# The first turn of an experts' loop written out ahead of it, and its end laid out anew, in a decoder step on one Trainium2 core

## The chip, the core and the metric

The kernel runs on one core of one Trainium2 chip. Its engines run side by side, each with its own list of instructions: TensorE (PE; its weight loads are listed apart as PEld), VectorE (DVE), ScalarE (ACT), GpSimd (POOL) and SyncE (SP), which here only issues DMAs. They wait for each other by semaphores. The metric is the device time of one execution in microseconds, as the median of several runs.

## What is computed

The reference is one step of a hybrid decoder layer for 256 prompt tokens and 64 sample tokens (8 sequences of 8): adaptive norm, an input projection, retention and mLSTM heads, an output projection, then a mixture of experts. What matters here is the last part:

```python
logits = x @ w_router + b_router              # 320 tokens, 32 experts
gates = softmax(top_4(logits))
for e in range(32):                           # the tokens that chose expert e
    hu = xe @ w_up[e] + b_up[e]               # 1024 -> 2048
    gate, lin = min(hu[:, :1024], 7), clip(hu[:, 1024:], -7, 7)
    y = ((lin + 1) * gate * sigmoid(1.702 * gate)) @ w_down[e] + b_down[e]
    out[tokens] += gates[tokens, e] * y
x = x + gt_f * out                            # per token scale
y_final = rms_norm(x, g_final)
```

All 32 experts' weights, 12 MB each in float32, are read from HBM once.

## The kernel before

Before the loop, TensorE and the other engines do norm, projections, heads and router, and leave the normed tokens as three bfloat16 parts (`h2p`) whose sum is the float32 value. `counts_i` holds how many tokens chose each expert. The work of an expert is built for four sizes, 32, 64, 96 or 128 token slots; `by_size` compares the count and jumps to one of four copies of the code.

**The loop** runs over the experts as one body of code per engine (`expert` of TensorE at L1117, called at L1210). On TensorE a turn `e` is: the down product of expert `e - 2` (L1063; `BEHIND` is 2, so that the first two turns leave it out by a branch at L1119), two count loads, the up product of expert `e` (L1039: 4 pieces of w_up, for each piece the matmuls of L1048, then the bias matmuls of L1052), the gather of expert `e + 1` (`gather`, L1001: 72 matmuls of L1008 that pick the chosen tokens with a one-hot matrix, in a copy for up to 64 slots and one for 128), the scatter of expert `e - 2` into the token order (L1106), the turning of the activations (L1058) and of the gate weights (L1114). In turns 0 and 1, in which there is nothing to scatter, `fill` (L513) puts 14 or 3 matmuls without use in its place (L1136). A float32 matmul of the code is two records in the trace: the up product of 32 slots is 64 records of L1048 and 4 of L1052, that of 96 slots 192 and 12. The code of 64 and of 128 slots has as many matmuls as that of 32.

The first gather is a routine of its own (`gather_first`, L985), ordered by the arrival of the parts, 9 groups of 8 matmuls. After it TensorE waits for `counts_ready` and enters the loop.

**SyncE** issues the weights in an order that is written out by hand (L465 to L479): all of expert 0, w_up of expert 1, then in turn `e` the four w_up pieces of expert `e` (`load_ups`, 2 MB each) and the four w_down pieces of expert `e - 1` (`load_downs`, 1 MB each). There is one place for each piece, so each issue waits until the product that last read this place is done: w_up of expert 1 for the up product of turn 0, w_up of expert 2 for that of turn 1, w_down of expert 1 for the down product of expert 0, which runs in turn 2.

**ScalarE** in a turn makes the sigmoid, copies the gathered tokens (`copy_gathered`, L1479), the gate weights (`copy_weights`, L1515), the turned activations to `actT` (`copy_turned`, L1499, which waits until the down product before has read `actT`) and the down product's result to `yd` (L1530).

**The end.** After the loop TensorE runs the down product of expert 30 (L1212) into banks 6 and 7, and `last_expert` (L1166): the gate weights of expert 31, its down product into the same banks, hence after ScalarE has copied `yd`. Halfway through this product it does the scatter of expert 30 (`scatter_before`, L1172: samples, then the two prompt tiles). When it is done, VectorE and ScalarE copy the result out, and the scatter of expert 31 follows: samples (L1188), then tiles 0 and 1 (L1193). VectorE's `finish` (L2207) adds the three tiles to the residual, the samples first, and after all three scales each by its `rstd` and `g_final` (L2240); ScalarE sums the squares (L1546), GpSimd makes the `rstd` (L1598, L1599), SyncE stores each tile. The `g_final` load (L1541) is issued by ScalarE after its copies.

Of the kernel before, what the change touches and what calls it, by code (L numbers as in the profile page):

```python
# [13 lines left out]
D = 1024  # L14
# [71 lines left out]
def build(nc, a):  # L86
# [6 lines left out]
    with ctx:  # L93
# [128 lines left out]
        yd_last = at(2 * SLOT, 2, 512); G_last = at(2 * SLOT + D, NTOK)  # L222
        assert o5 + 7168 + 1536 <= WORDS, o5 + 8704
# [284 lines left out]
        def _(pe):  # L508
# [475 lines left out]

            def gather_first():  # L985
# [13 lines left out]
                last.then_inc(S("gathered"), 1)  # L999

            def gather(i, count, turned, e=None):  # L1001
# [12 lines left out]
                if count is None:  # L1014
                    products(128)
                    return
# [46 lines left out]
            def down(it, slots, meanwhile=None):  # L1063

                end = meanwhile is not None
# [9 lines left out]
                for u in range(2):  # L1075
                    pe.matmul(psum[0:slots, 6 + u, :], bsel_down[:, 0:slots],
                              bparts[:, 2 * D + 512 * u:2 * D + 512 * u + 512], start=True, stop=False)
                last = [None] * DOWN
                for j in range(pieces):
                    if end and j == pieces // 2:  # L1080
                        meanwhile()
                    for u in range(2):
                        for q in range(tiles):
                            piece = q * pieces + j
                            c = piece // 2
                            if slots == 96:
                                turned = actT.rearrange("p j s -> p (j s)")[:, 0:8 * slots] \
                                    .rearrange("p (j s) -> p j s", j=KD)[:, piece, :]
                            else:
                                turned = actT[:, j, slots * q:slots * q + slots]  # L1090
# [5 lines left out]
                            last[c] = pe.matmul(psum[slots * q:slots * q + slots, 6 + u, :], turned,  # L1096
# [19 lines left out]

            def expert(e):  # L1117
# [48 lines left out]
            def last_expert(its, count):  # L1166
# [3 lines left out]
                turn_weights(its, 1)  # L1170

                def scatter_before():  # L1172

                    pe.wait_ge(S("G_ready"), its + 1)
                    pe.wait_ge(S("y_copied"), its + 1)
                    for u in range(2):
                        pe.matmul(psum[64 * u:64 * u + 64, 0, :], G[:, tok(2)], yd[:, u, :], start=True, stop=False)
                    pe.wait_ge(S("y_gated"), 2)
                    for t in range(2):
                        for u in range(2):  # L1180
                            pe.matmul(psum[:, 2 + 2 * t + u, :], G[:, tok(t)], yd_gated[:, u, :], start=True, stop=False)

                pe.wait_ge(S("y_copied"), its + 1)
                by_size(pe, count, lambda slots: down(its - 1, slots, scatter_before))
                pe.wait_ge(S("G_ready"), its + 2)
                for u in range(2):
                    pe.wait_ge(S("y_copied"), its + 2 + u)
                    last = pe.matmul(psum[64 * u:64 * u + 64, 0, :], G_last[:, tok(2)], yd_last[:, u, :], start=False, stop=True)  # L1188
                last.then_inc(S("last_scattered"), 1)
                pe.wait_ge(S("y_gated"), 4)  # L1190
                for t in range(2):
                    for u in range(2):
                        last = pe.matmul(psum[:, 2 + 2 * t + u, :], G_last[:, tok(t)], yd_last_gated[:, u, :], start=False, stop=True)  # L1193
                    last.then_inc(S("last_scattered"), 1)
# [4 lines left out]
            gather_first()  # L1199
            pe.wait_ge(S("counts_ready"), 1)  # L1200

# [4 lines left out]
            def count_at(i):  # L1206
                where = slice(i, i + 1) if isinstance(i, int) else bass.ds(i, 1)
                return pe.value_load(counts_i[0:1, where], min_val=0, max_val=NTOK)

            with pe.Fori(0, NE) as e:  # L1210
                expert(e)
            by_size(pe, count_at(NE - 1), lambda slots: down(NE - 2, slots))  # L1212
            most = pe.value_load(counts_i[0:1, NE + 2:NE + 3], min_val=0, max_val=NTOK)
            with pe.If(most <= BIG_BLOCK):
                last_expert(NE, count_at(NE))
            with pe.Else():
# [5 lines left out]
                last_expert(NE * ROUNDS, None)  # L1222
# [3 lines left out]
        def _(act):  # L1226
# [272 lines left out]
            def copy_turned(it, slots, down_before):  # L1499
# [3 lines left out]
                if down_before:  # L1503
                    for c in range(DOWN):
                        act.wait_ge(piece_done[UP + c], it)
                if slots == 96:
                    by_piece = actT.rearrange("p j s -> p (j s)")[:, 0:n] \
# [5 lines left out]
                act.copy(actT.rearrange("p j s -> p (j s)")[:, 0:n], src).then_inc(S("actT_ready"), 1)  # L1513
# [12 lines left out]
            def expert(r, e, it, count, count_next):  # L1526
                take_up(r * (NE + 1) + e, it, count, count_next)
                copy_weights(it)
                by_size(act, count, lambda slots: copy_turned(it, slots, True))
                act.copy(yd.rearrange("p u n -> p (u n)"), flat(6, D)).then_inc(S("y_copied"), 1)  # L1530

            def last_expert(its):

                act.wait_ge(S("Pg_turned"), its + 1)
                act.copy(G_last, psum[:, 1, 0:NTOK]).then_inc(S("G_ready"), 1)
                for c in range(DOWN):
                    act.wait_ge(piece_done[c], its + 1)
                act.copy(yd_last[:, 0, :], psum[:, 6, :]).then_inc(S("y_copied"), 1)
                act.wait_ge(S("y_gated"), 3)
                act.copy(yd_last[:, 1, :], psum[:, 7, :]).then_inc(S("y_copied"), 1)  # L1540
                act.dma_start(gfin.rearrange("p u n -> p (u n)"), a["g_final"].partition_broadcast(128))\  # L1541
                    .then_inc(S("gfin_in"), 16)
# [20 lines left out]
            by_size(act, count, lambda slots: copy_turned(0, slots, False))  # L1563
# [6 lines left out]
            with act.Else():  # L1570
                with act.Fori(1, ROUNDS) as r:
# [166 lines left out]
        def _(dve):  # L1738
# [468 lines left out]
            def finish(its):  # L2207
# [16 lines left out]
                TT(yd_last_gated[:, 1, :], psum[:, 7, :], gateF_p[:, 512:D], ALU.mult).then_inc(S("y_gated"), 1)  # L2224
# [8 lines left out]
                for t in range(2):  # L2233
                    dve.wait_ge(S("last_scattered"), 2 + t)
                    TT(x2[:, t, :], x2[:, t, :], flat(2 + 2 * t, D), ALU.add).then_inc(S("x3_ready"), 1)
                dve.wait_ge(S("gfin_in"), 16)
                for i, t in enumerate(LAST_ORDER):
# [3 lines left out]
                        ALU.mult, ALU.mult).then_inc(S("y_final"), 1)  # L2241

# [93 lines left out]
```

## Time and profile before

| what | us |
|---|---|
| median of 3 runs | 1298.41 (1296.67 to 1298.94) |
| the profiled execution, its own time | 1295.37 |
| its span, first to last instruction | 1293.6 |
| TensorE busy | 1163.6 (90%) |
| VectorE, ScalarE, GpSimd busy | 375.8, 182.7, 72.0 |
| HBM read over the span | 459.78 MB, 360 GB/s |

In the rows below, times count from the start of the span. A row of the timeline has the start, the length, the engine, the line of the kernel, the operation, the tiles and the count; in brackets the idle time of the engine ahead of it and who ended it, where "issue" is time in which it waited for nothing that the profile shows. The granted clock of TensorE has two levels here, 1.00 and 0.50 of full speed. Branches and register loads are not in the rows.

### The profile page before, as it was taken

Reading aid. Unit: us, or ns where it says so; the run is one execution under the profiler, and the core shown is the slowest. Engines: PE = TensorE matmul, PEld = TensorE weight load, DVE = VectorE, ACT = ScalarE, POOL = GpSimd, SP = SyncE. Lnnn points to the kernel's source line nnn. Section 1 sums busy time; section 2 is a strip of 40 time slices with the busy share of each in tenths; the row PEclk is TensorE's granted clock in tenths of the full one; section 3 lists DMA queues with packets and bytes.
Section 4 is the critical chain, followed back from the end, with each engine's and each line's share of the span. In section 5 each row is a group of like instructions: output and inputs, shape, how many; then the busy total and the mean of one; then the engine's idle time right before and its main releaser. Section 6 shows DMA issues by size and latency. Waiting matters only on the chain.

```text
span 1293.6 us, 23349 instructions
## 1 busy us (share of the span) xinstructions
PE 1163.6 (90%) x8690; PEld 567.3 (44%) x8691; DVE 375.8 (29%) x819; ACT 182.7 (14%) x358; POOL 72.0 (6%) x178
## 2 busy tenths in 40 slices
PE   5999999996989999998999998999777889988986
PEld 4655447544335446443344544444223334343332
DVE  0164214848211222321222121142211221222235
ACT  3112232213010111110110110010100000110101
POOL 1010001431000000000000000000000000000001
PEclk9999999998899999998999999999879999989999
DMA  9944635883689999999999999999999999999992
GB/s 366 363 152 172 239 131 196 253 317 138 260 351 424 409 417 427 427 428 425 428 424 426 426 426 428 426 376 428 427 426 428 426 425 426 426 426 428 427 422 85
DMA packets 62481, 467.36 MB, mean 361 GB/s; under 512 B 6538, under 2 KB 24910, under 8 KB 26730
## 3 DMA queue, kind: packets, MB, share of 16 engines
q1 hardware_dynamic: 59770, 461.86, 86.7%
q10 hardware_dynamic: 2288, 4.37, 1.1%
q0 software_dynamic: 384, 0.59, 0.2%
q8 instruction: 28, 0.46, 0.1%
q14 instruction: 11, 0.09, 0.0%
HBM read 459.78 MB, written 6.42 MB: 360 GB/s over the span
## 4 chain that ended last, share of the span: by engine, by line
PE 58%; DMA 36%; DVE 2%; issue 2%; ACT 1%; POOL 0%; SPq 0%; ACTq 0%; POOLq 0%; DVEq 0%
DMA mem<-in_w_up 33%; PE psum L1048 20%; PE psum L1096 9%; PE psum L680 6%; PE psum L1106 5%; PE psum L661 3%; PE psum L1008 3%; PE psum L867 2%; PE psum L684 2%; DMA mem<-in_in_chunks 1%; PE psum L536 1%; DMA mem<-in_mod_chunks 1%; PE psum L1058 1%; PE psum L871 1%; PE psum L1052 1%
## 5 line engine op out<-in xcount | busy, mean ns | idle before, releaser
L1048 PE MATMUL psum<-mem 128*32 128x512 f32 (+2 forms) x2432 | 399.9, 628 | 74.0 <-DMA mem<-in_w_up 66.8
L1048 PEld LDWEIGHTS psum<-mem 128*32 128x32 f32 (+2 forms) x2432 | 133.7, 123 | 330.3 <-issue 203.4
L1096 PE MATMUL psum<-mem 128*32 128x512 f32 (+3 forms) x1024 | 207.8, 594 | 0.0
L2172 DVE TENSOR_SCALAR mem<-psum 128x256 f32<-128x256 f32 (+3 forms) x32 | 19.2, 601 | 542.6 <-PE psum L1052 542.6
L1106 PE MATMUL psum<-mem 128*128 128x512 f32 x360 | 143.1, 608 | 3.3 <-DVE mem L2173 2.2
L1096 PEld LDWEIGHTS psum<-mem 128*32 128x32 f32 (+3 forms) x1024 | 93.3, 127 | 87.4 <-issue 61.2
L2205 DVE TENSOR_TENSOR mem<-mem,psum 128x1024 f32<-128x1024 f32 (+1 forms) x90 | 94.1, 1045 | 95.8 <-PE psum L1106 95.8
L680 PE MATMUL psum<-mem 128*128 128x512 f32 x192 | 84.2, 595 | 0.0
L1008 PEld LDWEIGHTS psum<-mem 128*128 128x128 bf16 x2232 | 74.7, 99 | 19.4 <-issue 19.1
L1496 ACT ACTIVATE mem<-mem 128x256 f32<-128x256 f32 (+3 forms) x32 | 17.9, 561 | 451.0 <-DVE mem L2172 451.0
L1008 PE MATMUL psum<-mem 128*128 128x64 bf16 (+1 forms) x2232 | 78.4, 196 | 0.0
L1106 PEld LDWEIGHTS psum<-mem 128*128 128x128 f32 x360 | 49.0, 171 | 51.9 <-issue 47.3
L1700 POOL CAST mem<-mem 128x128 bf16 (+1 forms) x33 | 10.7, 324 | 937.5 <-PE psum L1096 894.2
L680 PEld LDWEIGHTS psum<-mem 128*128 128x128 f32 x192 | 36.0, 190 | 43.7 <-issue 43.6
L2143 DVE TENSOR_SCALAR mem<-mem 128x128 bf16<-128x128 f32 (+1 forms) x99 | 22.2, 281 | 69.2 <-issue 69.2
L1513 ACT COPY mem<-psum 128x256 f32<-128x256 f32 (+2 forms) x29 | 14.0, 484 | 189.1 <-PE psum L1096 189.1
L661 PE MATMUL psum<-mem 128*128 128x320 f32 x128 | 36.7, 447 | 2.1 <-DMA mem<-in_in_chunks 2.1
L1246 ACT COPY mem<-psum 128x320 f32<-128x320 f32 (+9 forms) x65 | 25.0, 395 | 95.4 <-PE psum L680 68.1
L1519 ACT COPY mem<-psum 128x320 f32<-128x320 f32 x32 | 13.7, 428 | 155.9 <-PE psum L1106 147.7
L536 PE MATMUL psum<-mem 128*32 128x128 f32 x768 | 25.0, 286 | 7.8 <-DMA mem<-in_mod_chunks 6.9
L1530 ACT COPY mem<-psum 128x1024 f32<-128x1024 f32 x31 | 31.5, 1018 | 0.0
L661 PEld LDWEIGHTS psum<-mem 128*128 128x128 f32 x128 | 25.0, 197 | 13.1 <-DMA mem<-in_in_chunks 2.2
(279 smaller groups left out, 803.4 us busy)
## 6 DMA issues: line engine op xcount, KB each, us to landing
mem<-in_w_up SPq DMA_DIRECT2D x128, 2048.0 KB, 22.3
mem<-in_w_down SPq DMA_DIRECT2D x128, 1024.0 KB, 15.9
mem<-in_mod_chunks SPq DMA_DIRECT2D x12, 2048.0 KB, 12.3
mem<-in_in_chunks SPq DMA_DIRECT2D x8, 2048.0 KB, 9.9
mem<-in_out_chunks SPq DMA_DIRECT2D x2, 2048.0 KB, 10.0
mem<-in_x_prompt ACTq DMA_DIRECT2D x2, 1024.0 KB, 6.9
mem<-in_state_ret SPq DMA_DIRECT2D x4, 512.0 KB, 8.7
mem<-in_state_mlstm_c SPq DMA_DIRECT2D x4, 512.0 KB, 7.7
```

Of the source, the lines that this page charges most:

```text
L536: last = pe.matmul(psum[32 * t:32 * t + 32, bank, 0:128], cT[:, k, :], w[:, k, 128 * t:128 * t + 128], start=(k == 0), stop=False)
L661: last = pe.matmul(psum[:, q % BANKS, 0:NTOK], w[:, k, 128 * m:128 * m + 128], hT[:, k, :], start=(k == 0), stop=(k == KD - 1))
L680: last = pe.matmul(psum[:, q % BANKS, :], hT[:, k, tok(t)], w[:, k, :], start=(k == 0), stop=(k == KD - 1))
L684: last = pe.matmul(psum[64 * u:64 * u + 64, q % BANKS, 0:256], hT[:, k, tok(t)], w[:, k, 256 * u:256 * u + 256], start=(k == 0), stop=(k = ...
L867: last = pe.matmul(psum[:, 6 + u, :], hT[:, k, tok(t)], w[:, k, :], start=(k == 0), stop=(k == KD - 1))
L1008: last = pe.matmul(psum[:, 4 + k // 4, 128 * (k % 4):128 * (k % 4) + slots], h2p[:, part, t, dealt(k)], P[:, t, 0:slots], start=(part == 0 ...
L1048: last = pe.matmul(out, xg[:, 2 * c + h, cols], moving, start=(c + h == 0), stop=False)
L1096: last[c] = pe.matmul(psum[slots * q:slots * q + slots, 6 + u, :], turned, place(c, 2, D)[:, piece % 2, 512 * u:512 * u + 512], start=(j = ...
L1106: last = pe.matmul(out, G[:, tok(t)], yd[:, u, :], start=True, stop=True)
L1246: act.copy(*pairs[-1]).then_inc(S("evacuated"), 1)
L1530: act.copy(yd.rearrange("p u n -> p (u n)"), flat(6, D)).then_inc(S("y_copied"), 1)
L2205: TT(v, v, src, ALU.add).then_inc(S("added"), 1)
```

## The change

- *First turn.* TensorE's turn 0 is written out as `expert_first`, between the first gather and the loop, with constants in place of the loop's register and without the branches on `e`: up product, gather of expert 1, the 14 fills, turned activations, turned weights. The loop starts at 1. The two count loads are made inside `gather_first`, ahead of the last group of matmuls. `fill` in the loop has 3 matmuls always.
- *End, ScalarE.* Its loop stops one turn earlier, and that turn is written out (`expert_usual_end`): the gathered copy falls away, the activations go to a buffer of their own, `actT_last`, without waiting for the down product before, and that wait stands ahead of the copy to `yd`. `g_final` is loaded ahead of the last two copies.
- *End, TensorE.* The last down product goes to banks 4 and 5, waits for no copy of `yd`, and isn't cut in halves. Then follow the samples and tile 0 of expert 30, the samples and tile 0 of expert 31, then tile 1 of both. Tile 1 is added up in banks 6 and 7.
- *End, VectorE.* Tile 0 is added, then the samples scaled, then tile 1 added, then tiles 0 and 1 scaled.

The core of the diff (left out: new arguments of `down`, `gather` and `copy_turned`, and the path for experts of more than 128 tokens):

```diff
+        actT_last = at(2 * SLOT + 2 * D, KD, 128)
...
                 for part in range(3):
                     for t in range(NT):
+                        if part == 2 and t == NT - 1:
+                            pe.wait_ge(S("counts_ready"), 1)
+                            first_counts = count_at(1), count_at(2)
                         pe.wait_ge(S(f"part{part}"), t + 1)
...
+            def expert_first(count, count_next):
+
+                by_size(pe, count, lambda slots: up(0, 0, slots))
+                gather(1, count_next, 1)
+                pe.wait_ge(S("gate_ready"), 1)
+                pe.wait_ge(S("lin_clipped"), 1)
+                pe.nop().then_inc(S("scattered"), 1)
+                pe.nop().then_inc(S("scattered"), 1)
+                fill(14, 6)
+                pe.wait_ge(S("xg_ready"), 3)
+                by_size(pe, count, lambda slots: turn_activations(0, slots))
+                pe.wait_ge(S("added"), 1 + CLEARED)
+                turn_weights(0, 2)
+                pe.nop().then_inc(S("scattered"), 1)
...
-                    with pe.If(e < 1):
-                        fill(14, 6)
-                    with pe.Else():
-                        fill(3, 6)
+                    fill(3, 6)
...
-                pe.wait_ge(S("y_copied"), its + 1)
-                by_size(pe, count, lambda slots: down(its - 1, slots, scatter_before))
+                by_size(pe, count, lambda slots: down(its - 1, slots, True, acts))
+                pe.wait_ge(S("G_ready"), its + 1)
+                pe.wait_ge(S("y_copied"), its + 1)
...
+                samples(G, yd, True)
+                pe.wait_ge(S("y_gated"), 2)
+                prompt(0, G, yd_gated, True)
                 pe.wait_ge(S("G_ready"), its + 2)
+                samples(G_last, yd_last, False).then_inc(S("last_scattered"), 1)
                 pe.wait_ge(S("y_gated"), 4)
+                prompt(0, G_last, yd_last_gated, False).then_inc(S("last_scattered"), 1)
+                prompt(1, G, yd_gated, True)
+                prompt(1, G_last, yd_last_gated, False).then_inc(S("last_scattered"), 1)
...
-            gather_first()
-            pe.wait_ge(S("counts_ready"), 1)
...
-            with pe.Fori(0, NE) as e:
+            expert_first(*gather_first())
+            with pe.Fori(1, NE) as e:
                 expert(e)
...
+            def expert_usual_end(count):
+
+                by_size(act, count, lambda slots: sigmoid(NE - 1, slots))
+                act.wait_ge(S("gathered"), NE + 1)
+                act.nop().then_inc(S("xg_ready"), 1)
+                copy_weights(NE - 1)
+                by_size(act, count, lambda slots: copy_turned(NE - 1, slots, actT_last))
+                down_before(NE - 1)
+                act.copy(yd.rearrange("p u n -> p (u n)"), flat(6, D)).then_inc(S("y_copied"), 1)
...
-            with act.Fori(1, NE) as e:
+            with act.Fori(1, NE - 1) as e:
                 expert(0, e, e, count_at(e + 1), count_at(e + 2))
             most = act.value_load(counts_i[0:1, NE + 2:NE + 3], min_val=0, max_val=NTOK)
             with act.If(most <= BIG_BLOCK):
+                expert_usual_end(count_at(NE))
                 last_expert(NE)
...
+                add_last(0)
+                dve.wait_ge(S("gfin_in"), 16)
+                scale(0)
+                add_last(1)
+                scale(1)
+                scale(2)
```

## Rows read from the trace of the kernel before

**Rows 1.** The page: DMA load in 40 slices (part 2), the chain's shares by engine (part 4).

```profile
DMA  9944635883689999999999999999999999999992
...
PE 58%; DMA 36%; DVE 2%; issue 2%; ACT 1%; POOL 0%; SPq 0%; ACTq 0%; POOLq 0%; DVEq 0%
```

**Rows 2.** The chain of waits in order of time: start us, length us, what.

```profile
539.56 23.04 DMA mem<-in_w_up
...
1218.60 25.65 DMA mem<-in_w_up
```

**Rows 3.** Stretches: length, busy (count) of PE, PEld, DVE, ACT, POOL; clock, DMA share, GB/s.

```profile
440.00:442.00 2.00, 1.91 (x9) 0.65 (x10) 0.85 (x3) 1.49 (x3) 0.60 (x2) 1.00 0.43 94
...
324.24:328.40 4.16, 4.16 (x20) 0.97 (x24) 2.27 (x7) 0.00 (x0) 0.00 (x0) 0.50 0.03 6
328.40:345.00 16.60, 16.60 (x158) 4.61 (x153) 0.00 (x0) 0.00 (x0) 0.00 (x0) 0.99 0.73 274
...
325.34:338.78 13.44, 13.44 (x112) 3.52 (x108) 1.21 (x5) 0.00 (x0) 0.00 (x0) 0.87 0.44 166
```

**Rows 4.** The timeline of the first turn, from the first gather to the second up product.

```profile
317.61 0.62 PE L996 MATMUL psum<-mem 128*128 128x128 bf16 x8 [0.22 <-DVE mem L2089]
318.27 0.59 ACT L1554 COPY mem<-psum 128x512 f32<-128x512 f32 x1 [0.39 <-PE psum L996]
...
319.88 1.28 ACT L1496 ACT_TABLE_LOAD   x1 [1.02 <-issue]
...
321.81 0.87 PE L1048 MATMUL psum<-mem 128*32 128x512 f32 x1 [3.58 <-issue]
...
324.24 22.64 PE L1048 MATMUL psum<-mem 128*32 128x512 f32 x188 [1.56 <-issue]
...
347.89 2.28 PE L1008 MATMUL psum<-mem 128*128 128x64 bf16 x72
...
352.49 2.94 PE L517 MATMUL psum<-mem 128*128 128x256 bf16 x14 [2.31 <-issue]
...
357.72 7.07 PE L1048 MATMUL psum<-mem 128*32 128x512 f32 x64 [0.79 <-ACT mem L1519]
```

**Rows 5.** Instruction queues in 311:357, 357:1258 (q14 alone), 321.9:322.0, 325.3:325.4, 349.0:349.1, 1258.3:1258.4.

```profile
q8 instruction: 7, 0.11, 0.9%
...
q14 instruction: 1, 0.01, 0.0%
...
q8 instruction: 1, 0.02, 58.3%
...
q8 instruction: 1, 0.02, 85.8%
...
q8 instruction: 1, 0.02, 60.4%
...
q8 instruction: 1, 0.02, 67.9%
```

**Rows 6.** The timeline of the end, from the last down product but one.

```profile
1255.42 0.38 PE L1076 MATMUL psum<-mem 128*64 128x512 bf16 x1
...
1263.52 1.02 ACT L1530 COPY mem<-psum 128x1024 f32<-128x1024 f32 x1
...
1265.29 0.38 PE L1076 MATMUL psum<-mem 128*64 128x512 bf16 x1 [1.84 <-ACT mem L1530]
...
1278.58 1.47 PE L1188 MATMUL psum<-mem 128*64 128x512 f32 x4 [1.18 <-ACT mem L1538]
...
1279.98 3.70 PE L1193 MATMUL psum<-mem 128*128 128x512 f32 x8
...
1289.03 1.29 DVE L2240 SCALAR_TENSOR_TENSOR mem<-mem 128x1024 f32<-128x1024 f32 x1 [0.71 <-POOL mem L1599]
```

**Rows 7.** The timeline of the second turn: its fills, and the first down product behind it.

```profile
367.98 0.50 PE L517 MATMUL psum<-mem 128*128 128x256 bf16 x3 [0.76 <-issue]
...
371.43 0.60 PE L1076 MATMUL psum<-mem 128*96 128x512 bf16 x2 [1.74 <-issue]
```

More of the change, by code:

```diff
@@ L983, in _, with count_at @@
             turn_rows(2)
+            def count_at(i):
+                where = slice(i, i + 1) if isinstance(i, int) else bass.ds(i, 1)
+                return pe.value_load(counts_i[0:1, where], min_val=0, max_val=NTOK)
             def gather_first():
@@ L1015, in gather @@
                     products(128)
+                    return
+                if e is None:
+                    with pe.If(count <= 64):
+                        products(64)
+                    with pe.Else():
+                        products(128)
                     return
@@ L1061, in turn_activations, with down @@
                 last.then_inc(S("act_turned"), 1)
-            def down(it, slots, meanwhile=None):
-                end = meanwhile is not None
+            def down(it, slots, end=False, acts=actT):
+                first = 4 if end else 6
                 def place(c, *shape):
@@ L1075, in down @@
                 for u in range(2):
-                    pe.matmul(psum[0:slots, 6 + u, :], bsel_down[:, 0:slots],
+                    pe.matmul(psum[0:slots, first + u, :], bsel_down[:, 0:slots],
                               bparts[:, 2 * D + 512 * u:2 * D + 512 * u + 512], start=True, stop=False)
@@ L1095, in down @@
                                     pe.wait_ge(piece_in[UP + c], 16 * (it + 2))
-                            last[c] = pe.matmul(psum[slots * q:slots * q + slots, 6 + u, :], turned,
+                            last[c] = pe.matmul(psum[slots * q:slots * q + slots, first + u, :], turned,
                                                 place(c, 2, D)[:, piece % 2, 512 * u:512 * u + 512],
@@ L1164, in expert_later, with last_expert @@
                 by_size(pe, count_before, lambda slots: down(it - 1, slots))
-            def last_expert(its, count):
+            def last_expert(its, count, acts):
                 pe.wait_ge(S("G_ready"), its + 1)
@@ L1170, in last_expert, with samples @@
                 turn_weights(its, 1)
-                def scatter_before():
-                    pe.wait_ge(S("G_ready"), its + 1)
-                    pe.wait_ge(S("y_copied"), its + 1)
+                by_size(pe, count, lambda slots: down(its - 1, slots, True, acts))
+                pe.wait_ge(S("G_ready"), its + 1)
+                pe.wait_ge(S("y_copied"), its + 1)
+                def samples(weights, rows, first):
                     for u in range(2):
[L1177 to L1181, printed above, removed]
@@ L1183, in last_expert, with prompt @@
-                pe.wait_ge(S("y_copied"), its + 1)
-                by_size(pe, count, lambda slots: down(its - 1, slots, scatter_before))
+                        if not first:
+                            pe.wait_ge(S("y_copied"), its + 2 + u)
+                        last = pe.matmul(psum[64 * u:64 * u + 64, 0, :], weights[:, tok(2)], rows[:, u, :],
+                                         start=first, stop=not first)
+                    return last
+                def prompt(t, weights, rows, first):
+                    for u in range(2):
+                        last = pe.matmul(psum[:, (2, 6)[t] + u, :], weights[:, tok(t)], rows[:, u, :],
+                                         start=first, stop=not first)
+                    return last
@@ L1528, in expert, with down_before @@
                 copy_weights(it)
-                by_size(act, count, lambda slots: copy_turned(it, slots, True))
+                by_size(act, count, lambda slots: copy_turned(it, slots, actT, True))
+                act.copy(yd.rearrange("p u n -> p (u n)"), flat(6, D)).then_inc(S("y_copied"), 1)
+            def down_before(it):
+                for c in range(DOWN):
+                    act.wait_ge(piece_done[UP + c], it)
+            def expert_usual_end(count):
[5 more added lines that the diff above has]
+                down_before(NE - 1)
                 act.copy(yd.rearrange("p u n -> p (u n)"), flat(6, D)).then_inc(S("y_copied"), 1)
```

54 lines of the change are left out of this document (21 added, 33 removed).

## The prediction

> **What bounds the kernel now.** I read the page first, then the chain, then the stretches in which the load on DMA breaks off. The page's row of DMA load shows the 16 engines full from the thirteenth slice to the last but one, while the chain's summary gives TensorE 58% of the span and DMA 36% [rows 1]. The chain tells how these follow each other: up to 539.56 us it is matmuls in every turn of the experts' loop, from there to the thirty-second turn it is nearly always a wait of some 25 us for a w_up piece [rows 2]. From that alone a microsecond of TensorE before 540 us looks lost in the stream of weights. It isn't. The stream can only start once the first turn's up product frees the pieces, and it runs dry once more, at 440 to 442 us, where its share is 0.43 [rows 3]: there it waits for TensorE. So what TensorE gains or loses between the first gather and 440 us moves every later load, and with them the end, one for one. The stretch after the last load is TensorE and VectorE alone. The change touches just these two places: the first turn and the end.
>
> **The first turn as it is.** Its up product is late for what it needs. The last eight matmuls of the first gather run from 317.61, ScalarE's copy of them from 318.27 to 318.86, and then TensorE's first up matmul comes at 321.81, after 3.58 us put down to "issue"; after that single matmul there is a second such gap of 1.56 us [rows 4]. Behind the gaps the granted clock is 0.50, and 20 matmuls take 4.16 us, where 158 later ones take 16.60 (0.105 each) [rows 3]: 2.1 us lost. The fills wait 2.31 us, also for "issue" [rows 4]. These gaps stand beside instruction packets: queue 8, by its times TensorE's, brings seven of 16 KB between 311 and 357 us, among them one at 321.9 and one at 349.0, and in the 900 us after that the answer has no row of queue 8 at all [rows 5]. So the loop's code is read once, in the first turn, in step with its use, and stays. From packet to first use it takes 2.3 us (321.9 to 324.24). [...]
>
> **The parts.** (a) *First up product.* Two count loads move ahead of the gather's last tile. Their price is bounded by ScalarE, which makes the same two loads and a choice of size between 318.27 and 319.88: 1.6 us [rows 4]; below by nothing. About 1.0 us of it lies in the wait for that tile's rows, so the tile and both copies come 0.6 us later, and the up product starts at 318.86 + 0.6 + 0.2 = 319.65. It starts 2.15 us earlier, loses the second gap (2.3 us from 321.81 to 324.24, less its one matmul), since the code follows the gather in a straight line and the next block is asked for in time, and keeps its clock (2.1 us): its end is 6.5 us earlier, between 2.2 (both gaps come back elsewhere) and 6.5.
>
> (b) *Fills and the way into the loop.* The branches ahead of the fills go; the packet of the block that holds them comes 1.2 us after the gather begins (347.89, 349.0), as now, so they gain little: they may start 1.2 + 2.3 = 3.5 us after it instead of 4.6 [rows 4, 5]. What used to be a jump back to code already there is now an entry into code never read: the block with the second turn's counts, asked for when the fills' block is begun, costs 5.4, so 8.9 us after the gather's start; with the two count loads and the size (1.6 us) and the first instructions, the second up product starts 11.2 us after it, where now it is 9.8 (347.89 to 357.72) [rows 4]. This gives back 1.4 us; bounds are a gain of 2.3, if the fills' gap goes and nothing comes for it, and a loss of 2.
>
> (c) *The second turn runs cold.* Here lies the largest term, and no row of before has it, because now the second turn finds all code in place: its fills wait 0.76 us and its down product 1.74 us for "issue", with no packet [rows 5, 7]. After the change its code is read for the first time. It has 32 slots (64 matmul records at 357.72), so from its up product it jumps over those for 64, 96 and 128 slots. By the code's loops these are 68, 204 and 68 matmuls and as many weight loads: 680 instructions. [...] So three blocks in series, while the second turn's own loads keep DMA full. The first is covered by 2.5 us of queued matmuls, 5.4 - 2.5 = 2.9; the second by next to nothing, 5.1; the third by the rest of the gather and today's gap, 5.4 - 1.9 - 0.7 = 2.8. That is 10.8, and 1.0 for a clock that falls in such gaps (bounded by 0 and the first turn's 2.1): 11.8 us. Bounds: 4.6 at the idle price of 3.4 each, 15.
>
> On TensorE nothing follows that makes this good: the down product that frees the first expert's w_down pieces is next, SyncE's queue holds load_downs(1) behind that and load_ups(3) behind it, and the stream runs dry until then. To 440 us: -6.5 + 1.4 + 11.8 = **+6.7 us**. The other turns and their DMAs are as before; the fills and the branch taken out save nothing where e is 2 or more, since those turns never ran them.
>
> (d) *The end.* The last down product no longer waits for ScalarE's copy of yd (the copy starts 1263.52, the product 1265.29, 1.84 us idle): actT_last is written while the down product before still runs. Both halves run on, and the two scatters of the expert before follow them, so the copies out of banks 4 and 5 lie beside 3.3 us of matmuls: the 1.18 us ahead of the last samples' matmuls go too [rows 6]. TensorE's last matmul is 3.0 us earlier. Behind it hangs the same chain of VectorE, ScalarE and GpSimd as now, to the last scale at 1289.03. Tile 0 is done before tile 1's matmuls are, so its statistics no longer stand ahead of tile 1's on GpSimd; against that, VectorE's scale of the sample rows, with its waits for rstd3 and g_final, now stands before tile 1's addition, and at worst 1.3 us of it (the last scale's length) are added. I take 3.0, bounds 1.5 and 3.7. ScalarE's peeled last turn adds waits for `gathered` and, behind the copy of the activations, for the down pieces; queued behind these is the copy of yd alone, which has waited for the same matmuls all along. Moving the g_final load ahead of two copies costs at most its issue, long before the copies can start.
>
> **The sum**: 6.7 - 3.0 = +3.7 us on a profiled execution of 1295.37. That one lies 3.04 below the median, 1298.41, and I add it there: **1302.1 us**. What a measurement of this kernel can tell from no change is 0.2%, 2.6 us.
>
> **The rivals.** *The second turn finds its code in time* (the jump's block is fetched with the others, or code is read again in every turn anyway): the first up's 6.5 stays, the fills gain up to 2.3, the end 3.0. This gives -9.5 to -11.8, about 1288, faster. For it: straight code shows no gap at a block edge (13.44 of 13.44 us busy) [rows 3]. Against: 349.0 and 352.49, where a block one ahead was still late. It decides at the second turn's gather: no gap in front of it. Chance 0.16. [...] Chance 0.19, of which a third ends within 0.2%. *The end gains nothing*, because VectorE waits for the sample rows' rstd while tile 1 is ready: +6.7, 1305. For it: one engine does both; against: three groups of 1.85 us (half of the eight matmuls at 1279.98 each) lie between the samples' last matmul and tile 1's [rows 6]. Chance 0.10. My forecast has 0.55, of which a sixth falls within 0.2%.
>
> **The numbers.** Faster: 0.16 + 0.13 = 0.29; same: 0.06 + 0.09 = 0.15; slower: 0.46 + 0.10 = 0.56. The forecast's own range is 1298 to 1308 (cold turn 8 to 15, end 1.5 to 3.7). The range down to 1290 takes in the second rival, and leaves out most of the first and the top of the third: 1290 to 1308.
>
> **What would show it.** Right: the first up matmul near 319.7 with no second gap and the clock at 1.00; the second up product 11 us after the first turn's gather begins; then gaps of "issue" of 3, 5 and 3 us before, inside and after the second turn's gather, queue 8 packets beside each, DMA's share low for some 7 us before the first w_down(1) lands; the last down product without a wait, the last matmul 17.5 us after it starts. Wrong: a second turn without packets or gaps, or a stream of weights that never runs dry although TensorE is late.

## The result and the profile after

The changed kernel takes 1302.83 us (median of 18 runs, 1298.80 to 1306.81), the kernel before 1296.08 (18 runs, 1293.47 to 1302.38): ratio 1.0044, 95% interval 1.0030 to 1.0058. The profiled execution took 1302.98 with a span of 1301.1, 7.6 and 7.5 more than the one before. So the change makes the kernel slower by 6.75 at the medians. The forecast was 1302.1, but by a step of +3.7 from three runs whose median stood 2.3 above that of the 18: the side and the place of the loss were right, while all four terms came out beyond their bounds and cancelled in part.

On the page of after, the twelfth slice of DMA load (358 to 390 us) has 0.5 where [rows 1] has 0.8, and queue 8 has 32 packets where before has 28:

```profile
DMA  9935535973659999999999999999999999999993
...
q8 instruction: 32, 0.52, 0.2%
```

The timeline of TensorE in after, from the first gather's last tile to the third up product, answers to [rows 4, 7]:

```profile
316.60 0.62 PE L1004 MATMUL psum<-mem 128*128 128x128 bf16 x8 [0.55 <-DVE mem L2127]
318.20 20.81 PE L1063 MATMUL psum<-mem 128*32 128x512 f32 x192 [0.99 <-DVE mem L2302]
...
339.59 2.28 PE L1017 MATMUL psum<-mem 128*128 128x64 bf16 x72
343.94 1.69 PE L518 MATMUL psum<-mem 128*128 128x256 bf16 x14 [2.06 <-issue]
...
351.89 9.66 PE L1063 MATMUL psum<-mem 128*32 128x512 f32 x64 [5.13 <-issue]
...
366.12 0.98 PE L1017 MATMUL psum<-mem 128*128 128x64 bf16 x15 [4.35 <-issue]
371.26 3.15 PE L1017 MATMUL psum<-mem 128*128 128x64 bf16 x57 [4.16 <-issue]
379.16 0.80 PE L518 MATMUL psum<-mem 128*128 128x256 bf16 x3 [4.75 <-issue]
...
399.50 1.06 PE L1063 MATMUL psum<-mem 128*32 128x512 f32 x8
```

Turn 0 gains what it was to gain: both gaps ahead of the up product are gone, and the gather of turn 0 starts 8.3 us earlier (339.59, 347.89). Then follow 5.13 us without work ahead of the second up product, and three gaps of 4.35, 4.16 and 4.75 before, inside and behind the second turn's gather. The third up product starts at 399.50, in before at 385.70, so 13.8 later:

```profile
385.70 7.07 PE L1048 MATMUL psum<-mem 128*32 128x512 f32 x64
```

Beside the gaps stand the packets, each of which brings 16 KB of code (0.52 MB in 32), called a block below. Queue 8 in the stretches 311 to 357 (seven, as in [rows 5]) and 357 to 381 of after, where the four come at 363.2, 369.0, 375.8 and 378.9; in before the second stretch has none, and from 381 to 1270 after has none either:

```profile
q8 instruction: 7, 0.11, 0.9%
...
q8 instruction: 4, 0.07, 1.1%
```

The load on DMA differs from gap to gap (columns as in [rows 3], the granted clock and the DMA share stand ahead of the GB/s). In order: the gap ahead of the second up product, in which DMA is nearly idle, the one ahead of the gather and the one inside it, in which DMA is full, and the one behind it, in which the loads run out. The last row is the stretch from there into the first down product, with hardly any load:

```profile
346.90:351.90 5.00, 0.01 (x1) 0.01 (x1) 0.85 (x3) 1.10 (x3) 0.00 (x0) 0.84 0.05 16
361.80:366.10 4.30, 0.00 (x0) 0.00 (x0) 1.61 (x4) 0.42 (x1) 0.00 (x0) 0.75 1.02 431
367.10:371.30 4.20, 0.04 (x3) 0.04 (x2) 0.00 (x0) 0.00 (x0) 0.00 (x0) 0.50 1.00 419
374.40:379.20 4.80, 0.05 (x2) 0.07 (x2) 0.67 (x3) 0.59 (x1) 0.00 (x0) 0.84 0.64 266
...
375.00:389.00 14.00, 8.40 (x18) 3.68 (x19) 1.10 (x5) 0.47 (x2) 0.00 (x0) 0.63 0.18 73
```

The stretches of TensorE show what the gaps did to its clock (columns as in [rows 3], TensorE alone). After: up products of turns 0 and 1, the two parts of the second gather, the first down product, the third up product; then the stretch in which the stream of weights runs dry, which answers to the first of [rows 3]:

```profile
318.20:339.01 20.81, 20.80 (x196) 1.00 0.69 254
351.89:361.55 9.66, 9.65 (x68) 0.73 0.50 176
366.12:367.10 0.98, 0.98 (x15) 0.50 1.05 451
371.26:374.41 3.15, 3.15 (x57) 0.53 1.01 432
382.65:399.57 16.92, 16.92 (x38) 0.85 0.45 165
399.57:406.58 7.01, 7.01 (x69) 1.00 0.91 332
...
453.60:455.60 2.00, 1.91 (x9) 0.65 (x10) 0.85 (x3) 1.41 (x3) 0.60 (x2) 1.00 0.27 49
```

Before, in the same order, the second up product, the second gather and the first down product:

```profile
357.72:364.79 7.07, 7.07 (x68) 2.16 (x68) 0.27 (x2) 0.45 (x2) 0.00 (x0) 1.00 0.58 192
365.01:367.22 2.21, 2.21 (x72) 2.09 (x72) 1.61 (x4) 0.42 (x1) 0.00 (x0) 1.00 0.96 408
371.43:385.77 14.34, 14.34 (x38) 5.42 (x42) 0.00 (x0) 0.00 (x0) 0.53 (x2) 1.00 1.01 427
```

The stream still runs dry for TensorE after that (453.6, 13.6 later than 440 in before), and the chain goes over to the w_up loads 13.6 us later, at 553.15 instead of 539.56 [rows 2]. Only 0.2 of the 13.8 was taken up on the way.

The end answers to [rows 6]. Timeline of after from the last up product's bias matmuls:

```profile
1260.40 0.60 PE L1067 MATMUL psum<-mem 128*64 128x512 bf16 x4
...
1276.04 0.40 PE L1091 MATMUL psum<-mem 128*64 128x512 bf16 x1
...
1287.24 5.42 PE L1210 MATMUL psum<-mem 128*128 128x512 f32 x12
...
1296.74 1.29 DVE L2280 SCALAR_TENSOR_TENSOR mem<-mem 128x1024 f32<-128x1024 f32 x1 [0.93 <-POOL mem L1637]
```

I measure the end from the start of these bias matmuls to the end of VectorE's last scale: 42.5 us in before (1247.79 to 1290.32), 37.6 here (1260.40 to 1298.03). The last down product waits for nothing.

### The profile page after: what moved, and what is told of

Read it like the earlier page. It is cut to its first block, busy times and chain, and to the rows that moved or that the text cites. A ratio compares the mean times of both kernels' runs of the same rounds, so it can differ in the third digit from the quotient of the medians.

```text
span 1301.1 us, 23315 instructions
## 1 busy us (share of the span) xinstructions
PE 1160.3 (89%) x8688; PEld 560.7 (43%) x8691; DVE 376.3 (29%) x819; ACT 182.4 (14%) x357; POOL 71.1 (5%) x178
## 4 chain that ended last, share of the span: by engine, by line
PE 57%; DMA 36%; issue 3%; DVE 2%; ACT 1%; POOL 0%; SPq 0%; ACTq 0%; POOLq 0%; DVEq 0%
DMA mem<-in_w_up 34%; PE psum L1063 20%; PE psum L1109 9%; PE psum L681 6%; PE psum L1119 5%; PE psum L1017 3%; PE psum L662 3%; PE psum L868 2%; DMA mem<-in_mod_chunks 2%; PE psum L685 2%; PE psum L537 1%; PE psum L1127 1%; PE psum L872 1%; PE psum L1073 1%; ACT mem L1428 1%
## 5 line engine op out<-in xcount | busy, mean ns | idle before, releaser
L1063 PEld LDWEIGHTS psum<-mem 128*32 128x32 f32 (+2 forms) x2432 | 128.5, 123 | 341.5 <-issue 207.0
L662 PE MATMUL psum<-mem 128*128 128x320 f32 x128 | 36.7, 448 | 2.0 <-DVE mem L1798 2.0
L2192 DVE TENSOR_SCALAR mem<-mem 128x128 f32<-128x128 f32 (+1 forms) x99 | 28.3, 343 | 11.5 <-PE psum L1127 7.6
L662 PEld LDWEIGHTS psum<-mem 128*128 128x128 f32 x128 | 25.0, 197 | 13.1 <-DMA mem<-in_in_chunks 2.1
```

The source lines that it names most:

```text
L662: last = pe.matmul(psum[:, q % BANKS, 0:NTOK], w[:, k, 128 * m:128 * m + 128], hT[:, k, :], start=(k == 0), stop=(k == KD - 1))
L1063: last = pe.matmul(out, xg[:, 2 * c + h, cols], moving, start=(c + h == 0), stop=False)
L2192: last = TSC(Pg[0:n, t, :].rearrange("p (q s) -> p q s", s=slots), sl[0:n, :].unsqueeze(1).to_broadcast([n, 128 // slots, slots]), pos[0:n ...
```

## The experiments

All differences between turns are taken from the end of the first gather's last eight matmuls (318.23 in before, 317.23 in after), since that point lies anywhere from 317 to 327 in these executions, mostly by work that the edits don't touch (e5, e6 and e10 also have edits ahead of it). Single executions still differ behind it: the third up product starts 67.5 after that point in before, but 72.0 in e1 and 68.5 in e7, which have before's code there. So a difference of 4.5 or less in this measure proves nothing. The profiled executions of e1, e3 and e9 took 4.8, 6.3 and 6.5 more than their medians.

**Each half alone.** e1 has the new end and the loop from turn 0; e2 the written-out first turn and the old end. Together they are the diff shown; against after, e1 undoes this (and `expert_first`, the early count loads and the choice of 14 or 3 fills with it), e2 all the rest:

```diff
-            expert_first(*gather_first())
-            with pe.Fori(1, NE) as e:
+            gather_first()
+            pe.wait_ge(S("counts_ready"), 1)
+            with pe.Fori(0, NE) as e:
                 expert(e)
```

> The new end on the kernel before, with its loop from turn 0. If the end is worth what the trace of after shows behind the last up product (from the last bias matmul to the last scale 42.5 us before, 37.6 after, so 4.9): first turn as before, that stretch 37.6 again, time 1296.1 - 4.9 = about 1291, ratio 0.996. Rival, the end gains only the 3.0 us forecast or less, and the rest of what after made good came from the stream of weights: 1293 to 1296, stretch 39.5 or more.

> The written-out first turn with the old end. Theory (the second turn reads its code cold): the third up product starts some 15 us later behind the first gather than before, the three gaps of 4 to 5 us stay, the stream passes nearly all of it on, and nothing is made good at the end: 1296.1 + 11.7 to 13 = about 1308 to 1309, ratio 1.009. Rival (the stream takes up most of a late second turn, and the loss of after lies in the new end): 1296 to 1300.

e1: 1290.13 (1287.69 to 1297.49), ratio 0.9958 (0.9941 to 0.9975). e2: 1310.11 (1307.27 to 1312.31), ratio 1.0107 (1.0084 to 1.0129). The change is two changes of opposite sign. The stretch of the end is 37.6 in e1 and 42.3 in e2: it follows the end's code, whatever the first turn was; in e2 the three gaps of the second turn are 4.78, 4.21 and 4.66, and the third up product starts 80.3 after the first gather (82.3 in after, 67.5 in before). The two ratios multiply to 1.0065, beside 1.0044 for the whole, which the intervals allow. e1 has the lowest median of this study, below both kernels; e3 can't be told from it.

**Where the jumps lie.** e3, on e1, moves the down product to the end of the loop's body; the order of the work is the same:

```diff
-                with pe.If(e >= BEHIND):
-                    by_size(pe, count_two_back(e), lambda slots: down(e - 2, slots))
-                with pe.Else():
-                    pe.nop()
                 count, count_next = count_at(e + 1), count_at(e + 2)
...
+                with pe.If(e >= 1):
+                    by_size(pe, count_at(e), lambda slots: down(e - 1, slots))
+                with pe.Else():
+                    pe.nop()
...
-            by_size(pe, count_at(NE - 1), lambda slots: down(NE - 2, slots))
```

> New end; no turn written out; in TensorE's loop the down product moves from the start of turn e to the end of turn e - 1, so that the first gather is followed by the up product's code with no jump over the down product's. Theory (a forward jump past the blocks held is what costs): the two gaps at the first up product (3.58 and 1.56) shrink to the count loads, about 2, and the second goes; from turn 2 on no packets; instead a gap of 3 to 5 at the end of turn 0, where the down product is jumped over, and up to 5 more when it first runs in turn 1. Up product 0 ends 4 to 6.5 earlier, 3 to 8 come back: 1286 to 1293, near 1290. Rival (turn 0's gaps come from waits for other engines): the same gaps stay in front of the first up product, and the time is that of the new end alone, 1291.

The chain of e3 through turn 0 and into turn 1:

```profile
324.47 0.93 issue
325.40 2.76 PE psum L1049 x19
...
328.43 18.45 PE psum L1049 x169
...
356.25 4.03 issue
360.28 9.63 PE psum L1049 x64
...
370.13 2.21 PE psum L1009 x72
372.34 0.76 issue
```

As expected: with no jump past the down product ahead of it, the first up product ends 24.4 after the gather (29.7 in before); the jump now stands at the end of turn 0, and there is the gap of 4.03, and behind it the second up product takes 9.63 at a granted clock of 0.73, in before 7.07 at 1.00. The first run of the down product cost 1.26, no more than in before. The second turn has no gap at its gather, though the first up product is early: the gaps of after don't come from that. The time, 1291.22 (ratio 0.9962, 0.9941 to 0.9982), is that of e1, so it does not decide; the trace does.

e4 takes after and lays the loop's four copies of the up product out in reverse, 128 slots first (conditions turned about, same copies):

```diff
-                by_size(pe, count, lambda slots: up(e, e, slots))
+                by_size_down(pe, count, lambda slots: up(e, e, slots))
```

> After, with the four copies of the loop's up product laid out from 128 slots down to 32, so that the copy for 32 slots is followed at once by the gather. The work is the same. Theory (the jump past 64, 96 and 128 slots makes the gather's code late): the 4.35 us ahead of the second turn's gather fall under 1.5, and the 4.66 ahead of the second up product grow by 2 to 5, since the jump past three copies now stands there; total within 3 of 1302.8. Rival (TensorE waits there for data of another engine, or for a block edge that lies at the gather anyway): both gaps stay as they are within 0.5.

The chain of e4 around the second up product and the gather behind it:

```profile
353.86 11.19 issue
365.05 8.95 PE psum L1063 x64
...
374.21 2.21 PE psum L1017 x72
376.42 3.58 issue
```

The gap ahead of the gather and the one inside it are gone, the one behind it is 3.58, and 11.19 stand ahead of the up product: 6.5 more, beyond the 2 to 5. The gap moved with the jump, though the work was the same and its data no earlier. This rules out a wait for another engine at the gather. In sum the reversed order is no dearer: the third up product starts 76.5 after the first gather, 5.8 sooner than in after, little more than single executions differ by. The first gather ended 7.0 later in this execution, so that the time of the one run, 1303.01, says nothing on this.

**Twice the cold code.** e8 writes out the second turn too, as `expert_first` with its numbers one higher and 3 fills:

```diff
             expert_first(*gather_first())
-            with pe.Fori(1, NE) as e:
+            expert_second(count_at(2), count_at(3))
+            with pe.Fori(2, NE) as e:
```

> After, with the second turn written out as well, so that the loop starts at turn 2. Theory (each stretch of code is paid at its first run, the more so behind a jump): the second turn keeps a gap of 3 to 5 at its gather, and the third turn (down product, up product, gather, scatter for the first time) gets gaps of 3 to 5 at two to four places, where after has none; the fourth up product starts 8 to 18 later than in after: 1311 to 1320. Rival (the second turn is late for its data, in whatever code it stands): the gaps stay in the second turn alone, 1301 to 1305.

e8's chain in the second and third turn:

```profile
360.39 5.39 issue
365.78 2.37 PE psum L1017 x41
368.14 3.46 issue
...
404.13 10.92 issue
415.05 6.39 PE psum L1017 x72
```

The second turn, now straight code behind the first, has only 0.52 ahead of its up product, but keeps its gaps at the gather; the third turn gets one of 10.92 where after has none (one place instead of two to four). The fourth up product starts 6.2 later than in after, less than the 8 I gave; one run took 1312.83. Packets come with it: ten from 358 to 460 us, where after has four from 357 to 381 and then none. In this one execution the loss grows with the code that is read for the first time.

**The jump made early.** e5, on e1, puts the first gather into the loop, in the branch that turn 0 takes anyway; e6 does the same with the routing of the third tile and the places ahead of it (`before_first`, in e6 alone):

```diff
                 with pe.If(e >= BEHIND):
                     by_size(pe, count_two_back(e), lambda slots: down(e - 2, slots))
                 with pe.Else():
-                    pe.nop()
+                    with pe.If(e < 1):
+                        before_first()
+                        gather_first()
+                        pe.wait_ge(S("counts_ready"), 1)
+                    with pe.Else():
+                        pe.nop()
```

> New end; no turn written out; the first gather moves into the loop, to the branch of turn 0 that leaves out the down product. So the jump past the down product's code is made before the first gather, and the gather's code is followed by the up product's. The second turn is as before. Theory (a late block of code behind a jump is what costs): the jump's block costs up to 3.4 ahead of the gather, where TensorE has some time; the first up product starts 1 to 2.7 after the gather (the two count loads) with no second gap, and ends 24 to 25 after the gather's end, where it is 29.7 in before; no gap over 1 at the second turn's gather: 1290.1 - 5, less what the gather is late, 1284 to 1289. Rival (the written-out code isn't the cause, the second turn's gaps follow from an early first up product): they appear here too, 1295 or more. Second rival (the longer loop is no longer kept): packets of queue 8 through all turns, 1310 or more.

> As the run before, but the loop is entered earlier still: the third tile's routing and the places go into the branch of turn 0 too, so that the jump past the down product's code lies beside a wait of 2.7 for VectorE. Theory: the same first up product (24 to 25 after the gather's end), and the gather isn't late: 1283 to 1287. Rival (longer loop not kept): packets of queue 8 in later turns, 1310 or more.

Both missed. e5 took 1294.02 (ratio 0.9980, 0.9963 to 0.9998), 3.9 above e1 at the medians. No gap stands at the second gather (0.75 behind it), which speaks against the first rival, but the jump cost 1.85 ahead of the first gather, which ends 9.2 after the matmuls before it (5.8 in before), and another 3.59 stand ahead of the first up product, where I had 1 to 2.7. That product ends 27.4 after the gather instead of 24 to 25.

e6 took 1345.14 (ratio 1.0367, 1.0329 to 1.0406): the rival of the longer loop came true. The page's queue 8:

```profile
q8 instruction: 53, 0.87, 0.3%
```

Two pieces of e6's chain, where before has none:

```profile
705.12 5.44 issue
...
861.72 5.98 issue
```

Its loop is longer by the routing's matmuls than e5's, whose queue 8 has 28 packets as before; from 470 to 1000 us e6 has 12 packets, where before has none. So e6's loop is not kept, while those of before and e5 are (no packet from 357 to 1258 and from 360 to 1262). That length decides is the likely reading, but not shown: no run changes the length alone, and e9, below, gets packets again in two turns from a loop that is only moved.

**The same code, moved.** e9 lays 41 instructions that never run ahead of after's loop; e10 lays 100 empty ones at TensorE's start, on e1 (the second part of the diff).

```diff
+                with pe.If(count >= NTOK):
+                    for _ in range(40):
+                        pe.nop().then_inc(S("pad"), 1)
...
+            for _ in range(100):
+                pe.nop().then_inc(S('pad'), 1)
             pe.wait_ge(S("tables_in"), 16)
```

> After, with 41 instructions that never run laid ahead of TensorE's loop (a branch on a count of 320, which no expert has, around 40 empty instructions). In after the gap inside the second turn's gather comes behind 15 matmuls and 15 weight loads, so behind some 30 instructions. Theory (the gap is the edge of a block of code): moved by 41 instructions, the edge lies ahead of the gather, among code that is jumped over: the 4.16 us inside the gather go, and the gather's 72 matmuls take 2.2 to 3.2 us in one piece; the gaps ahead of the gather (4.35) and behind it (4.75) stay within 1.5: the third up product 3 to 6 earlier behind the first gather, 1297 to 1300. Rival (a wait for another engine, or for the DMA engines, in the midst of the gather): the three gaps as in after, 1301 to 1304; the edges lie elsewhere by chance in either case at no more than 1 us in steady turns.

> The new end on the kernel before, with 100 empty instructions ahead of everything on TensorE, where it waits for the first load anyway. In the kernel before, a gap (1.56) comes behind the very first matmul of the first up product, so the edge of a block lies two instructions into it. Theory: the edge moves 100 instructions away from that product's start; the second gap (1.95 with the new end) goes, and with it a part of the cold clock behind it, while the first (3.1 to 3.6) stays; the gap ahead of the fills (2.3 to 2.5) moves into the gather or stays: 1290.1 - 2 to -4 = 1286 to 1288. Rival (position doesn't matter): 1290.

e9's chain, second to fourth turn:

```profile
367.60 4.21 issue
371.81 3.54 PE psum L1017 x72
375.35 2.39 issue
...
405.19 4.49 issue
409.67 4.62 PE psum L1017 x50
414.29 0.86 issue
...
449.66 2.66 issue
```

The gap inside the second gather went, as it should if it was the edge of a block, and the gap ahead of the gather stayed (4.21). The one behind it did not stay within 1.5, as I had it: it fell from 4.75 to 2.39. The third up product starts 8.8 sooner after the first gather than in after. But the third turn, which takes the gather's copy for 128 slots, and the fourth have gaps that after has not, with packets beside them (7 from 385 to 450). Total 1304.44, ratio 1.0068 (1.0046 to 1.0091): 1297 to 1300 was wrong. That position decides where TensorE waits is shown; that I can say beforehand how much it adds up to is not. Whether these packets bring code of the second turn again, and why, is open.

e10 took 1303.73 (ratio 1.0062, 1.0041 to 1.0082), 13.6 above e1. The 100 instructions weren't hidden: TensorE's first matmul comes at 16.21, at 8.38 in e1, and the first of L664 at 44.1, where the same line (L662) starts at 34.9 to 37.8 in all other runs. So 6 to 9 of the 13.6 lie there; whether the instructions' own time or another block to be read makes them is not shown. The second gap is gone (the up product is one piece of 192 matmuls), but the first is 4.76, and new ones of 1.70 inside the gather, 0.93 and 1.05 behind it and 2.35 ahead of the second up product stand in its place. Moving code there gained nothing.

**The end, without VectorE's new order.** e7 is e1 with both additions ahead of the scales:

```diff
                 add_last(0)
+                add_last(1)
                 dve.wait_ge(S("gfin_in"), 16)
                 scale(0)
-                add_last(1)
```

> The new end on the kernel before, but VectorE makes both additions before it scales the samples. If the order tile by tile is worth something, the stretch from the last bias matmul to the end of the last scale (42.5 in before, 37.6 with the new end) is 38.0 to 39.5; if all of the gain comes from TensorE's matmuls being earlier, it stays at 37.6; if the order costs something, as I had it (the scale of the samples ahead of tile 1's addition, at worst 1.3), it falls to 36.3.

One run took 1293.03. The stretch is 37.9 (1249.57 to 1287.44), between the two values expected: VectorE's order is worth 0.3 of the 4.9 (the stretch is 37.6 in after, e1, e3 and e5 alike). The rest comes with the new order on TensorE and ScalarE, which no run takes apart.

## Why the forecast held, and where it didn't

Step by step, on the two profiled executions, with what ran ahead of the first gather's last tile taken out (it was 1.45 earlier in after: VectorE's part of it ends at 316.12, at 317.57 in before). Each number is from one execution.

| step | forecast | measured |
|---|---|---|
| (a) end of the first up product | -6.5 | -6.85 |
| (b) gather of turn 0 to second up product | +1.4 | +2.5 |
| (c) second up product to third: gaps | +10.8 | +12.5 |
| (c) the same: clock | +1.0 | +7.1 |
| to the third up product | +6.7 | +15.2 |
| (d) the end | -3.0 | -4.9 |

(a) was right in its parts too, and 0.35 past its bound of 6.5: the tile came 0.44 later behind VectorE (0.6 forecast), the up product started 2.2 earlier, and ran at 1.00.

(b) was over its bound of 2: the fills' gap went down only from 2.31 to 2.06, and the entry into the loop cost 4.66 of "issue" behind ScalarE's copy. From the packet's row I had 3.5 from the gather to the fills; it was 4.35. I had also taken the loop's first block at 5.4, asked for when the fills' block is begun. No run shows either. Queue 8 has packets at 347.2 and 350.8 ahead of the second up product, with DMA's share at 0.05 (346.90 to 351.90). Less the 1.6 taken for the count loads and the size, 4.66 leaves some 3.1 by estimate.

(c) The three gaps in series are there, before, inside and behind the gather, each with a packet in it (363.2, 369.0, 375.8; the last has that of 378.9 too), and 2.9, 2.2 and 3.4 from these three to the next matmul; the one inside the gather stands behind 15 matmuls and 15 weight loads, some 30 instructions. In sum they cost about what was forecast: 4.35, 4.16, 4.75, less the 0.76 that before had, is 12.5 for 10.8. Singly they are off: 4.35, 4.16 and 3.99 for 2.9, 5.1 and 2.8. The terms of that sum are shown by no run: neither the 5.4 for each of three blocks and the 3.4 of the lower bound (e5's expectation has it too, and 1.85 was measured there), nor the 2.5 us of queued matmuls that were to cover the first. What the traces have is the gaps and the packets, and 220 matmuls and weight loads between the packets at 325.3 and 338.8 of before [rows 3], 259 between those at 321.8 and 335.2 of after, both stretches without a gap. The rival that finds the code in time falls by the gaps and by e2, e3 and e4, the second, whose sum is the lower bound of 4.6, by the size of the sum (12.5), though not every gap lay under full DMA. The one in which the end gains nothing falls by e1.

What failed is the clock term, 1.0 with an upper bound of 2.1: the second up product lost 2.6 (9.66, 7.07), the gather 1.9 (4.13, 2.21), the first down product 2.6 (16.92, 14.34). The bound came from one gap of turn 0; here four gaps follow each other, and the granted clock is back at 1.00 only in the third up product. That the second up product's loss belongs to the gap ahead of it is borne out by all twelve traces: it takes 7.07 or 7.08 where at most 0.79 stand ahead of it (before, e1, e5, e7, e8), and 8.77 to 9.85 where 2.27 to 11.66 do (after and the other six). The 2.6 of the down product can't be laid on the cold code alone: e1, whose second turn has no such gaps, shows the same product at 0.84 and 17.13, while in e7, with e1's code there, 32 of its matmuls take 13.73 as in before (15.86 in after). How much of the clock's loss is due to the change stays open to that extent. The term as a whole, 19.6 for 11.8, lies past its bound of 15, and DMA's share was low for 14 us (375 to 389), not 7.

That code stays in place once read held as well: no queue 8 from 381 to 1270 in after, as from 357 to 1258 in before. That a jump past code not yet read makes what follows it late is borne out by e3 and e4, where the gap goes with the jump (4.03 and 11.19 us). How much code TensorE keeps is not shown: seven packets of 16 KB come from 311 to 357 in before, and the next 900 us have none [rows 5].

What I reasoned about the stream (what TensorE loses ahead of 440 us moves the end, one for one) held: +13.8 at the third up product, +13.6 at 553, +12.6 at the last up product; 1.0 went in the weight stream between the last two, the only part that was not passed on.

(d) was mis-sized, and past its bound of 3.7. The last matmul came 3.6 earlier, counted from the bias matmuls (32.3 instead of 35.9): 1.9 at the down product's start, 1.8 after it, where I had 1.2. Behind the last matmul I had taken the chain as unchanged; it is 5.4 instead of 6.6, since tile 0 is through by then and only one tile is left. By e7 the order on VectorE made 0.3 of that.

The net, +15.2 - 4.9 - 1.45 ahead of it - 1.0 in the stream, is 7.8, as the two executions differ by 7.6, where the forecast had 3.7. The errors are +8.5 in (a) to (c), -1.9 in (d) and -2.4 outside the change; at the medians (6.75) 3.0 of error is left, of which before's later median, 2.3 under the one I had added to, cancelled most. So the number was better than its terms: each of the four lies past its bound, and that the sum came within 0.7 of the measured median was luck.

## What to carry to other kernels

Writing a loop's first turn out ahead of it doesn't only save that turn's branches: the loop's own code is then read for the first time one turn later, where it cost four gaps of 4 to 5 us here; count its code and the jumps past unused copies before doing it. Here three gaps were forecast at their places, but not what a change of position adds up to (e9, e10). A loop whose code is kept can also lose that by an edit that looks harmless: one tile's routing moved into it cost 3.7% (e6). Where an edit has two independent halves, time each by itself: here one was worth -0.42% and the other cost +1.07%.

## What was not expected of the hardware

- A loop's code can stop being kept, and this shows in single turns: e6 has 12 packets and gaps such as 5.44 and 5.98 (at 705 and 862 us) between 470 and 1000 us, where before has neither, and takes 1.0367 times as long.
- TensorE's clock stayed down in after, where gaps follow each other: the granted clock is 0.73, 0.50 (the lower level throughout), 0.53 and 0.85 in the stretches from 351.89 to 399.57, and 1.00 in the next. The last of these stretches, the down product, has a lower clock in some executions without such gaps too (0.84 in e1).
- One hundred empty instructions with a semaphore increment each, at a place where TensorE seemed to wait for a load, put the first matmul 7.8 us later (16.21, 8.38).
